# Down-projection passes in another order: two plain pieces ahead of the first block product, one amid them, one ahead of the last

## The reference

```python
def swiglu(h, w_gate_up, w_down):
    gu = jnp.einsum('bsd,df->bsf', h, w_gate_up)
    gate, up = jnp.split(gu, [FFN_HIDDEN], axis=-1)
    return jnp.einsum('bsf,fd->bsd', jax.nn.silu(gate) * up, w_down)
...
        gu = hn @ w_up[l]
        g = _dwconv_centred(gu[..., :D_FF], ffn_conv_w[l], ffn_conv_b[l])
        u = gu[..., D_FF:]
        f = (jax.nn.gelu(g, approximate=True) * u) @ w_down[l]
        h = h + _rmsnorm(f, post_ffn_gain[l])
```

## Time and profile before

| | us |
|---|---|
| median of 3 runs | 2674.47 (2674.43 to 2675.14) |
| the profiled execution | 2673.37 |
| its span, first to last instruction | 2671.6 |
| PE busy in the span | 2640.9 (99%) |
| DVE busy | 1856.3 (69%) |
| ACT busy | 1303.7 (49%) |

### The profile page before, as it was taken

How to read it: one execution, slowest core, us unless ns; L and a number is a source line. 1 busy time by engine, 2 the same in 40 slices (tenths; PEclk the granted TensorE clock), 3 DMA queues, 4 the chain that set the end, 5 groups by cost and what they waited for, 6 DMA issues and landing times.

```text
span 2671.6 us, 37118 instructions
## 1 busy us (share of the span) xinstructions
PE 2640.9 (99%) x13950; PEld 2272.8 (85%) x13950; DVE 1856.3 (69%) x1881; ACT 1303.7 (49%) x1313; POOL 3.5 (0%) x8
## 2 busy tenths in 40 slices
PE   9999999999999999999999999999999999999998
PEld 8888888888888888888888788888888888888877
DVE  7646666665555556875558768888777787677877
ACT  6544444444445444444445556645554454444444
POOL 0000000000000000000000000000000000000000
PEclk9999999999999999999999999999999999999999
DMA  7555555455555555555554554543555546555553
GB/s 250 189 189 174 174 187 188 173 190 190 218 191 179 189 188 206 198 204 184 189 188 162 191 194 172 178 151 133 199 173 188 188 161 217 194 188 189 186 211 134
DMA packets 71871, 497.23 MB, mean 186 GB/s; under 512 B 8183, under 2 KB 9432, under 8 KB 12648
## 3 DMA queue, kind: packets, MB, share of 16 engines
q1 hardware_dynamic: 71784, 496.06, 52.9%
HBM read 493.93 MB, written 2.10 MB: 186 GB/s over the span
## 4 chain that ended last, share of the span: by engine, by line
PE 93%; DVE 4%; ACT 1%; issue 1%; DMA 1%; DVEq 0%; SPq 0%; ACTq 0%
PE acc L2261 37%; PE acc L2269 19%; PE acc L2317 10%; PE acc L2493 7%; PE acc L2324 5%; PE acc L2498 3%; PE acc L2342 2%; DVE w_lo L1285 2%; PE acc L2338 2%; PE acc L2336 2%; PE acc L2365 1%; ACT w_hi L735 1%; PE acc L2620 1%; PE acc L2372 1%; PE aux L2761 1%
## 5 line engine op out<-in xcount | busy, mean ns | idle before, releaser
L1285 DVE TENSOR_TENSOR w_lo<-raw,w_hi 128x2048 fp32r<-128x2048 f32 (+1 forms) x467 | 1063.0, 2280 | 342.7 <-ACT w_hi L735 315.4
L735 ACT ACTIVATE w_hi<-raw 128x2048 fp32r<-128x2048 f32 (+1 forms) x467 | 889.4, 1906 | 801.6 <-PE acc L2261 337.2
L2261 PE MATMUL acc<-xa,w_hi 128*128 128x512 f32 x4480 | 1071.4, 391 | 0.2 <-ACT w_hi L735 0.2
L2261 PEld LDWEIGHTS acc<-xa,w_hi 128*128 128x128 f32 x4480 | 824.3, 188 | 161.8 <-issue 1.1
L2269 PEld LDWEIGHTS acc<-xa,w_lo 128*128 128x128 f32 x4480 | 574.1, 191 | 23.6 <-DVE w_lo L1285 2.0
L2269 PE MATMUL acc<-xa,w_lo 128*128 128x256 f32 x4480 | 581.6, 283 | 1.2 <-DVE w_lo L1285 1.2
L1297 DVE TENSOR_TENSOR tmp<-acc,small 128x512 f32<-128x512 f32 x120 | 82.9, 691 | 234.9 <-ACT small L745 234.4
L2317 PE MATMUL acc<-w_hi,hid 128*128 128x512 f32 x768 | 182.6, 390 | 0.0
L2493 PE MATMUL acc<-w_hi,xa 128*128 128x512 f32 x768 | 182.3, 390 | 0.0
L2317 PEld LDWEIGHTS acc<-w_hi,hid 128*128 128x128 f32 x768 | 143.8, 188 | 29.8
L2493 PEld LDWEIGHTS acc<-w_hi,xa 128*128 128x128 f32 x768 | 143.8, 188 | 29.7
(11 more groups left out here) (379 smaller groups left out, 2097.9 us busy)
## 6 DMA issues: line engine op xcount, KB each, us to landing
raw<-in_w_in SPq DMA_DIRECT2D x158, 1024.0 KB, 4.9
raw<-in_w_gate_up SPq DMA_DIRECT2D x88, 1024.0 KB, 4.9
raw<-in_w_down SPq DMA_DIRECT2D x88, 1024.0 KB, 4.9
raw<-in_w_up SPq DMA_DIRECT2D x87, 1024.0 KB, 4.9
raw<-in_w_out SPq DMA_DIRECT2D x32, 1024.0 KB, 4.9
raw<-in_w_uq SPq DMA_DIRECT2D x3, 1024.0 KB, 4.9
h_tok<-in_x_tok SPq DMA_DIRECT2D x1, 2048.0 KB, 9.3
raw<-in_w_ukv SPq DMA_DIRECT2D x4, 512.0 KB, 3.5
```

What stands on the lines that cost most here:

```text
L735: act.activation(hi_part(u, run)[:, 0:kt * P], raw_of(u)[:, 0:kt * P], ACT.Copy).then_inc(hi_made, splits(u, run))
L1285: dve.tensor_tensor(lo_part(u, run)[:, 0:kt * P], raw_of(u)[:, 0:kt * P], hi_part(u, run)[:, 0:kt * P], ALU.subtract).then_inc(lo_made, sp ...
L2261: last = pe.matmul(acc[:, bnk], w_hi[:, u % SPLIT, k * P:(k + 1) * P], x[:, k0 + k], start=first and k == 0, stop=False)
```

## The change

**New order of a pass.** PE's order was P1, M1, M5, M2, P2, M6, M3, M7, P3, M4, MIXED, P4, P5, P6 (P for `PLAIN_`, M1 for `M_1`). It is now P1, P2, M1, M5, M2, P3, M6, M3, M7, MIXED, P4, M4, P5, P6. The constants are positions in that order, so the order of the pieces, `FREED_BY` and `NEXT_SLOTS` follow. The piece of P2 is now piece 4, in the slot that P1's low half frees.

**The other work.** `weight_sum` 2 goes from P1 to M1, 4 from M3 to M7, 1 (for the second pass) from P5 to P6. The output sums `added`, `out_part` and `out_sum_both` of the even column come at M4 in place of MIXED. In the second group of block 1 the squares, token halves and gains of a finished column move: those of column 1 to M7 and MIXED, those of columns 0 and 2 to P5. At the seam, `weight_sum` 1 stands behind the low half of form 1. The wait for the last snap is now in the middle of MIXED. The edit `u, run = u + run, 0` in both `split`s makes them take the new slot for form 1, where a loop would take the next one.

```diff
-PLAIN_1, M_1, M_5, M_2, PLAIN_2, M_6, M_3, M_7, PLAIN_3, M_4, MIXED, PLAIN_4, PLAIN_5, PLAIN_6 = range(FORMS)
+PLAIN_1, PLAIN_2, M_1, M_5, M_2, PLAIN_3, M_6, M_3, M_7, MIXED, PLAIN_4, M_4, PLAIN_5, PLAIN_6 = range(FORMS)
...
-B_11, B_22, B_12, B_21 = 1, 2, 3, 4
-PIECE_OF = {PLAIN_1: 0, M_1: B_11, M_2: B_21, M_3: B_22, PLAIN_2: 5, PLAIN_3: 6, MIXED: 7, PLAIN_4: 8, PLAIN_5: 9, PLAIN_6: 10,
+B_11, B_22, B_12, B_21 = 1, 2, 3, 5
+PIECE_OF = {PLAIN_1: 0, M_1: B_11, M_2: B_21, M_3: B_22, PLAIN_2: 4, PLAIN_3: 6, MIXED: 7, PLAIN_4: 8, PLAIN_5: 9, PLAIN_6: 10,
             M_7: B_12, M_4: B_21}
 
-FREED_BY = (None, None, None, None, PLAIN_1, M_1, PLAIN_2, M_3, M_7, PLAIN_3, M_4)
-NEXT_SLOTS = (2, 3, 1, 0)
+FREED_BY = (None, None, None, None, PLAIN_1, PLAIN_2, M_1, PLAIN_3, M_3, M_7, M_4)
+NEXT_SLOTS = (1, 2, 3, 0)
...
-                    if n == 5:
+                    if n == 6:
...
+                if isinstance(run, int):
+                    u, run = u + run, 0
...
+                        if g and form == PLAIN_5:
+                            v_square(2 * p)
                         split(u + form + 2)
-                        if g and p and form == PLAIN_2:
+                        if g and p and form == M_7:
                             v_square(1)
-                        if g and p and form == PLAIN_3:
+                        if g and p and form == MIXED:
                             both_high(1)
-                        if g and p and form == MIXED:
                             x_square(1)
-                        if g and form == PLAIN_4:
-                            v_square(2 * p)
-                        if g and form == PLAIN_6:
+                        if g and form == PLAIN_5:
                             both_high(2 * p)
                             x_square(2 * p)
...
-                        if g and p and form == PLAIN_2:
+                        if g and p and form == M_7:
...
                         if p or ahead < 1:
                             split(u + 2, run)
-                        if last and p:
-                            weight_sum(u0 + 2 * GT, 1)
                         total(t, run, 2)
                         dve.tensor_tensor(tmp[:, 0:2], tmp[:, 0:2], rstd2, ALU.mult).then_inc(gate_in, 1)
                         if p or ahead < 2:
                             split(u + 3, run)
+                        if last and p:
+                            weight_sum(u0 + 2 * GT, 1)
...
-                        if form == MIXED:
-                            added(2 * p, u, MIXED)
+                        if form == M_7:
+                            weight_sum(u, 4)
+                        if form == M_4:
+                            added(2 * p, u, M_4)
                         if form == PLAIN_6:
                             added(2 * p + 1, u, PLAIN_6)
                         split(u + form + 2)
-                        if form == PLAIN_1:
+                        if form == M_1:
                             weight_sum(u, 2)
                         if form == M_5:
                             snap(u, b_22, M_1, h_tok[:, 2 * p, 0])
                             snap(u, b_12, M_5, h_tok[:, 2 * p + 1, 1])
                         if form == M_2:
                             weight_sum(u, 3)
-                        if form == M_3:
-                            weight_sum(u, 4)
-                        if form == PLAIN_5 and p + 1 < PASSES:
+                        if form == PLAIN_6 and p + 1 < PASSES:
                             weight_sum(u + FORMS, 1)
-                        if g and p and form == PLAIN_3:
+                        if g and p and form == MIXED:
                             tokens_low(1, DT, V_LAT, gain)
-                        if g and p and form == M_4:
                             final_gain(1)
-                        if g and form == PLAIN_6:
+                        if g and form == PLAIN_5:
                             tokens_low(2 * p, DT, V_LAT, gain)
                             final_gain(2 * p)
...
-            def both_columns(u, t):
+            def both_columns(u, t, snap):
-                parts = ((20, b_11, b_21, False), (21, b_11, b_21, True), (20, b_12, b_22, False), (21, b_12, b_22, False))
+                parts = ((20, b_11, b_21), (21, b_11, b_21), (20, b_12, b_22), (21, b_12, b_22))
                 pe.wait_ge(hi_made, u + 1)
-                for k, (tile, *tiles, _) in enumerate(parts):
+                for k, (tile, *tiles) in enumerate(parts):
+                    if k == 2:
...
                 plain(PLAIN_1, b_11, 8, first=True)
+                plain(PLAIN_2, b_11, 12)
                 pe.wait_ge(acc_free, b_22 + 1)
                 product(u + M_1, b_22, *hidden(0, 0), first=True, final=True)
                 pe.wait_ge(x_sums_lo, 3 * (group + 1))
                 product(u + M_5, b_12, *sums_14(1), first=True, final=True)
                 product(u + M_2, b_11, *hidden(4, 0))
-                plain(PLAIN_2, b_11, 12)
+                plain(PLAIN_3, b_11, 16)
                 pe.wait_ge(snapped, snaps + 1)
                 product(u + M_6, b_22, *SUMS_2, final=True, more=True)
                 pe.wait_ge(snapped, snaps + 2)
                 product(u + M_3, b_12, *sums_14(0), more=True)
                 pe.wait_ge(snapped, snaps + 3)
                 product(u + M_7, b_22, *hidden(0, 1), final=True, more=True)
-                plain(PLAIN_3, b_11, 16)
-                product(u + M_4, b_21, *hidden(4, 1))
                 if p == 0:
                     pe.wait_ge(op_lo, v1 + GT)
-                pe.wait_ge(snapped, snaps + 4)
-                both_columns(u + MIXED, t)
+                both_columns(u + MIXED, t, snaps + 4)
+                if after:
+                    after(MIXED)
                 plain(PLAIN_4, b_12, 8)
+                product(u + M_4, b_21, *hidden(4, 1), final=True)
                 if not staggered:
                     plain(PLAIN_5, b_12, 12)
```

28 lines of the change are left out of this document (16 added, 12 removed), and 8 rows, old and new, of the table PIECES.

## The result

| | us | span, profiled | granted clock |
|---|---|---|---|
| before, median of 5 runs | 2674.43 (2673.43 to 2675.14) | 2671.6 | 0.999 |
| after, median of 5 runs | 2689.44 (2687.89 to 2690.94) | 2689.2 | 0.997 |

The change makes the kernel **15.0 us slower**, a ratio of 1.0057 with a 95% interval of 1.0042 to 1.0071. The forecast was 2681.7, its range ended at 2687.0. The sign was right, the size half of what came, and the time is 2.4 us above the range.

The account below looks back on a forecast made before the run. PE's own work was taken to set the time, so the change only moves stalls, 20.8 us in the passes before. +10.8 in the passes and -3.6 behind block 1 gave +7.2 on 2674.5: 2681.7 us, range 2675.5 to 2687.

Parts of the forecast that it names:

- The seam: First passes: P2 waits for the slot P1 frees, the gate chain behind it; 5.1 us in block 1, 7.0 and 8.5 in block 2.
- The small terms behind M1: First passes, after M1's late high half: its low half about 0.59 us late, then P3 0.64 behind its load.
- Behind block 1: After block 1's last pass: column 2's token halves and gains now stand at P5, gaining 3.6 us.
- Second passes: Late low halves and snaps: 0.7 us each in block 1, 1.4 and 0.6 in block 2; 3.4 in all.
- moves priced at nothing: Output sums at M4, weight sum 1 behind P2's low half, three loads in a row behind M4's low half: no cost.
- 5.12 us: Every load: from the end of the low half that frees its slot to its reader's start, read at one place.
- `first_out`: Block 2, group 0, inside MIXED: M7's copy waits behind P4's high half; 1.6 us in the first pass, 1.4 in the second.
- rival C: Half clock behind M1's 3 us stalls, some 1.7 us each; 2 to 4 of them give 2685 to 2688.5; 14%.
- Rival A: At the seams the load hides and the gate chain isn't late; all passes keep some 6.7 us of stalls, 2657; 7%.
- B: The seam costs as worked out, but small terms inside passes don't come: -5.4 us, giving 2676.3; 19%.

Follow-up runs that it names:

- Experiment 1: The changed kernel with weight sum 1 at the seam back ahead of the pair's total, nothing else; 2679.0 us.
- experiment 2: The changed kernel with the last pair's gate work ahead of P2's halves on ACT and DVE, the weight sum behind it all; 2667.29 us.
- experiment 5: The kernel before with only block 1, group 1's token halves, squares and gains of columns 0 and 2 at P5 instead of P6; 2667.72 us.
- experiment 11: The changed kernel with the last pair's gate work ahead of P2's half and `first_out` moved ahead, second-pass loads still three in a row; 2663.85 us.
- 7: The changed kernel with three repairs: last pair's gate work ahead of P2's half, `first_out` moved ahead, second-pass loads spread; 2658.76 us.
- experiment 10: The changed kernel once more, nothing edited; 2689.83 us in two runs.
- Experiment 3: The changed kernel with ACT's `first_out` of M7 (block 2, group 0) ahead of P4's high half; 2686.19 us.
- experiments 4: The changed kernel with second-pass loads spread: pieces 0 and 1 issued ahead of piece 10, at MIXED and P4; 2685.15 us.
- 8: The changed kernel with the first two pieces of each second pass loading 512 of 2048 columns; 2685.49 us.

## Why the prediction was half right

**The seam: right in its chain and its two large terms.** M1 was to be 3.04 late, 4.55 in block 2, group 1: PE idles 2.84, 2.85, 2.82 and 4.37. P2's low half 0.67 and 2.14: idle 0.32, 0.29, 1.78 and 1.75. The copy was to start 5.15 later than in the kernel before, with the pass at the same place; from P1's start it is 4.98 (1087.73 - 1082.50 = 5.23, before 0.25). Experiment 1 shows the 2.20 of the weight sum in it, experiment 2 the rest: the gate chain behind P2's half. The small terms behind M1 did less well: the 0.59 for its low half came as 0.16 at most, the 0.64 for P3 not at all at three seams and as 1.41 at one, behind a load of 6.1. So that the first passes add up to within 2.2 us of the forecast is in part luck: block 2, group 1 holds 6.3 without the clock for 8.8.

**Behind block 1: right.** Gain 3.6 predicted, 15.61 - 12.02 = 3.59 measured, and experiment 5 shows it alone, with a gain of 2.3 inside the last pass.

**Second passes: wrong, by the price of a landing.** Without the clock they hold 10.4 us for 3.4. Two steps failed. "Three loads in a row behind M4's low half (13 us ahead of P1)" stood among the moves priced at nothing. The cover I named was for those three loads. The price falls on the loads behind them, which take 6.1 to 10.9; P2's waits for them: 2.1 us in this trace, 2.9 in experiment 11 against 7. In the last pass, which holds most of it, the loads in a row are four, with `last_row`, which the prediction didn't count. And 5.12 us, read at one place, stood for every landing, where the same load takes about 4.9 or about 6.1 (experiment 10). P3's load is wanted with no slack in a second pass, so landings of 6.1 and 6.5 show in block 1: 1.1 and 1.4 us, which the sum had at nothing; 0.4 more in the last pass came with one of 4.9. Some 0.7 at M1 and 0.3 of small waits are the rest, with `first_out` below. The trace of before had both in it: its loads of 1121.9 and 1124.1, each issued 2.2 behind another, took 6.5 and 6.7.

The Trainium skill ("DMA: Bandwidth & Descriptors", Anatomy of one DMA) splits a DMA into a fixed part and one that grows with the bytes, by its fit for another issuing path an estimate of 2.4 us for 1 MB. The trace is near it where the queue is full: landings at 2619.2, 2621.6 and 2624.3, spaced 2.4 and 2.7.

**`first_out`: right in place, too small by the same step.** 1.6 and 1.4 predicted, idle 2.31 and 2.24 with loads of 6.1, 1.09 with one of 4.9. Experiment 3 shows that the copy ahead of P4's half costs nothing.

**The half clock: rival C, given 14%.** My sum let it go since one execution had it once and not behind its longest wait. After, it costs 6.8, before 1.7: +5.1 of the 17.6. In this trace it came behind waits of 2.24 us and more, and with M1's waits down to 2.16 at most (experiment 1) or gone (2) no pass had any. The Trainium skill's rule on PE-idle gaps ("TensorE: Matmul & The Clock Gate", Why this matters for your kernels) pointed this way; I read the one trace against it. The traces agree with it in part: behind 4.4 the clock fell each time, behind 3.08 not in the kernel before but in experiment 5, and it fell behind 1.56 in the kernel before and behind P2's wait of 1.8 at the third seam of experiments 4 and 8, gaps that the rule doesn't warn of. Experiment 10 shows that one trace can't speak against it: the same 2.85 fell once and once not. The price would have been an expected value, about 1.7 for each long wait times the share that falls, here 3 to 4 events. C's own number (up to 2688.5) comes near the measured time, but by luck: it has none of the loss in the second passes.

**The sum.** Predicted +7.2. To it come 6.9 in the second passes without the clock, +6.8 for the clock, -2.2 in the first passes, and -0.9 ahead of the first pass (1082.50 for 1083.42), which is chance, since other executions of the changed kernel begin it later: 7.2 + 6.9 + 6.8 - 2.2 - 0.9 = 17.8, against 17.6 between the traces. In the medians it is 15.0, as after's profiled execution lies 1.5 above its own median and before's 1.1 below. A's 6.7 and B's 5.4 of small terms are the same ones, which by the sum's own figures add up to 5.9; that changes neither.

Rival A asked for a landing within 1.2 us and a gate chain in time. The first never came; the second did in experiment 2, and with the loads spread the time was the 2658.8 that A (2657) had named: its shape was right for a kernel that this change isn't.
